# A float32 kernel of two transformer-like layers: convolution inputs turned by block transposes and transfers, a second queue of pieces, and smaller edits at the gates, the middle, the opening and the end

## The chip, the cores and the metric

The kernel runs on one core of a Trainium2 chip. The metric is the device time of one execution in microseconds, lower is better. A core has TensorE (PE in the profile; PEld is its weight load), VectorE (DVE), ScalarE (ACT), GpSimd (POOL) and SyncE (SP), which in this kernel issues nearly all DMA transfers.

## What is computed

A sequence of 256 tokens of width 2048, all in float32, goes through three blocks. The first is a gated MLP with mixing over tokens, the second a stick-breaking attention; neither is touched by the change, apart from the first instructions of the kernel. The third block is the one that matters here. Cut to its core, it is:

```python
xn = rmsnorm(x, norm_mix_pre)                       # 256 x 2048
mq, mk, mv, mo, mi, mf, aq, ak, av, g_m, g_a = split_cols(xn @ w_in)
# mq, mk, mv, mo, aq, ak, av: 1024 columns each; mi, mf: 4 each; g_m, g_a: 2048 each
qk = silu(causal_depthwise_conv(concat(mq, mk), conv_w, conv_b))   # 4 taps over tokens
h  = mlstm_chunkwise(*heads(qk), heads(mv), mi + i_bias, mf + f_bias)  # 4 heads of 256
h_m = rms_of_head(h) * mlstm_norm * sigmoid(mo)
h_a = attention(rope(aq), rope(ak), av)             # 8 heads of 128
merged = sigmoid(g_m) * (h_m @ w_branch_m) + sigmoid(g_a) * (h_a @ w_branch_a)
x = x + rmsnorm(merged @ w_out, norm_mix_post)
u = square(relu(rmsnorm(x, norm_ffn_pre) @ w_up))
x = x + rmsnorm(u @ w_down, norm_ffn_post)
```

The convolution is `out[t] = b + sum over j of w[j] * u[t - 3 + j]`, with zeros before the first token.

## The kernel before

**Matrix products in three passes.** Each float32 weight is split in two: the high half `t_wh` (written by ACT, line 42) and the low half `t_wl` (written by DVE, line 51, as the weight less its high half). Activations are held split and transposed, as `xth`/`xtl` (also `yth`/`ytl`, `mth`/`mtl`), and a product is the sum of three matmuls: low weights by high activations, high by high, and high by low. PE's work on them is line 33.

**Groups.** Weights come in groups of 128 x 1024 elements, 512 KB each, all in one order written in the program: SP loads a group to one of five buffers (`t_stage`), ACT and DVE split it into one of five pairs (`t_wh`, `t_wl`). Ahead of each group's matmuls `advance` emits the split of the group four later and the load of the next one. A load waits for the split that used its buffer, a split for the matmuls that used its pair. A usual group covers two row tiles of the activation and 512 columns of the weight, for two halves of the tokens (i = 0, 1): 12 matmuls. Eight such groups make a chunk of 512 output columns (`proj`). The gates have 8 columns only, 16 row tiles in two groups of 8 (`proj_gates`): there the weights, padded to 128 columns, are the stationary side and all 256 tokens are the moving side, three matmuls of 256 per row tile.

**Pieces.** All other work is cut into pieces, Python functions that emit instructions on the engines. They stand in a deque (`pieces`); `later(f, (g, 2), ...)` appends them, each with a least distance in groups from the piece before it, or from when it was queued. After each group `offer` emits the first piece if its distance has passed (and one more if over 18 stand in the queue); `need` emits pieces until a result that is wanted now is in the program. So the order on every engine is fixed when the program is built, and an engine that stands waiting in a piece holds back everything behind it on that engine, weight splits included.

**The third block before the change.** The order of chunks of `w_in` is: q columns of c = 0, gates, k columns of c = 0, v and o columns of c = 0, then q, k, v, o of c = 1, then q, k, v of the attention (c = 0, 1), then the branch products and so on. After each q or k chunk of the recurrent part `conv_t` queues four pieces. `first` (distance 2) transposes two 128 x 128 blocks for both halves of the tokens on PE (four transposes, line 36), ACT copies them behind three zero columns to `pad`, and DVE does the four taps of the first block (`tensor_scalar`, line 48, and three `scalar_tensor_tensor`, line 54). `second` does the taps of the other block, then ACT takes the tanh of half of it, and DVE multiplies (silu with a factor of two) into `vreg`. Both twice per chunk. The gates' pieces (`piece`, `gates_one` to `gates_five`) come from `gates_in`; the heads of the recurrence (`h0`, `h1`, `start`, `end`) are queued after the q, k, v and o chunks of a c. A rotary embedding is two pieces (`piece(0)`, `piece(1)`), the turn of its result for the attention a third (`turn_part`, which calls `send_heads`), and the scores follow five groups after them.

**Turning by block transposes.** Other chunks are already transposed without PE: `turn_chunk` makes 32 x 32 block transposes of both halves on DVE (line 39, `STREAM_TRANSPOSE`), and `send_turned` moves the blocks by four DMA transfers on SP to their places.

**Middle.** The last chunk of `w_out` is emitted so that its last three groups end with 18 matmuls for the first half of the tokens, then 18 for the second (`halves`, `late_groups=3`). Then come five small matmuls on constants, both square sums, the transposes of x (set up by `to_xt_now`), the norm and updates of the first half (`half_norm(0)`, `x3(0, 0, ..)`, `x3(1, 0, ..)`), the norm and updates of the second, and the products with `w_up`.

**End.** `last_norm(0)`, updates of chunks 0 to 2 of the first half, `last_sum(1)` (the last square sum), `update(3, 0)`, `last_norm(1)` and the updates of the second half.

**Opening.** ACT's first instruction is an activation on a zeroed tile; SP's first DMAs are `norm_g`, the first part of x (`load_x(0)`) and then weights and further parts of x in turn.

Of the kernel before, what the change touches and what calls it, by code (L numbers as in the profile page):

```python
# [16 lines left out]
D = 2048  # L17
# [162 lines left out]
def _program(nc, A, out, ctx):  # L180
# [30 lines left out]
    pad, _ = sb("pad", [128, 2, 260], offset=s_at + 4096)  # L211
    cpb, _ = sb("cpb", [128, 4 * 130], offset=s_at)
    ubuf, _ = sb("ubuf", [128, 2, 2, 512], offset=s_at)
    hold, _ = sb("hold", [8, S], offset=s_at + 4096 + 2112)
# [45 lines left out]
    pieces = deque()  # L260
    group_at = [0]
    pumped_at = [0]

    def pump():
        assert pieces, "nothing to pump"
        pumped_at[0] = group_at[0]
        pieces.popleft()[0]()
# [4 lines left out]

    def later(*fs):

        for f in fs:
            f, n = f if isinstance(f, tuple) else (f, 1)
            pieces.append((f, n, group_at[0]))
# [35 lines left out]
    AC.do(lambda e: e.activation(junk[:, 0:64], blank[:, 0:64], ACT.Copy), c_blank)  # L313
# [24 lines left out]
    def load_x(n):  # L338
        part = slice(256 * max(0, 2 * n - 2), 256 * max(1, 2 * n)) if n != 1 else slice(256, 512)
        x_in.append(SP.dma(lambda e: e.dma_start(hres[:, :, part], xin[:, :, part]), s_x[n], 16))  # L340
# [8 lines left out]
    load_x(0)  # L349
# [51 lines left out]
    def split_group(j):  # L401
        marks = (used[j - N_SPLIT],) if j >= N_SPLIT else ()
        s, r = j % N_STAGE, j % N_SPLIT
        src, hi, lo = stage[:, s], wh[:, r], wl[:, r]
        a = AC.do(lambda e: e.activation(hi, src, ACT.Copy), loaded[j], *marks)
        split_hi.append(a)
        split.append(DV.do(lambda e: e.tensor_tensor(lo, src, hi.bitcast(F32), ALU.subtract), a, *marks))
# [49 lines left out]
    def proj(xh, xl, k0, ready, halves=None, late_groups=1, high=None):  # L457
# [5 lines left out]
        for g in range(nk // 2):  # L463
# [24 lines left out]
            if halves is not None and g >= nk // 2 - late_groups:  # L488
                if g == nk // 2 - late_groups:
# [5 lines left out]
                    halves.append(mark)  # L495
                mark = group_products(xh, xl, k0, pair, n, nk, j, g, 1, ready, True)
# [47 lines left out]
    def proj_gates(xh, xl, ready):  # L544
# [5 lines left out]
        for g in range(2):  # L550
# [4 lines left out]
            for kk in range(8):  # L555
# [706 lines left out]
    def conv_t(src, mark, dst, base, marks, done):  # L1262
# [12 lines left out]
        for b in range(2):  # L1275
            s = {}

            def first(b=b, s=s):
# [16 lines left out]
                if b == 1:  # L1295
                    done(tp)
# [523 lines left out]
    for c in range(3):  # L1820
        update(c, 0)
# [61 lines left out]
```

How the kernel before makes its waits and increments, by code:

```python
    def wait(self, *marks):  # L87
        for sem, value in marks:
            if self.seen.get(sem.name, 0) < value:
                self.seen[sem.name] = value
                self.items.append(lambda e, s=sem, v=value: e.wait_ge(s, v))
# [1 line left out]
    def do(self, emit, *marks):  # L93
        self.wait(*marks)
        self.n += 1
        f = emit(BOUND)
        self.items.append(lambda e: f(e).then_inc(self.sem, 1))
        return (self.sem, self.n)
# [5 lines left out]
    def dma(self, emit, sem, value, *marks):  # L105
        self.wait(*marks)
        f = emit(BOUND)
        self.items.append(lambda e: f(e).then_inc(sem, 16))
        return (sem, value)
```

## Time and profile before

| | us |
|---|---|
| median of 3 runs (2595.32 to 2595.67) | 2595.36 |
| the profiled execution, its own time | 2595.48 |
| its span in the trace | 2593.7 |
| PE busy | 2583.2 (100%) |
| PEld busy | 2142.4 (83%) |
| DVE busy | 1599.8 (62%) |
| ACT busy | 1231.5 (47%) |
| POOL busy | 20.8 (1%) |

The span runs from the first to the last instruction of the trace; the execution's own time has 1.8 us more around it. Busy times are sums over the span. PE's weight loads overlap its matmuls. In rows of time order a matmul of 512 columns shows 0.39, since matmuls are pipelined; the distance from one to the next is 0.227. The DMA engines moved 203 GB/s on the mean. Where an engine sat idle before an instruction, the row has in brackets how long and which instruction released it.

### The profile page before, as it was taken

To read this page: it belongs to the slowest core of one execution; us is meant where nothing else is said; L and a number is where in the kernel's file an instruction comes from. 1 tells how busy PE (TensorE), PEld (TensorE's weight loads), DVE (VectorE), ACT (ScalarE), POOL (GpSimd) and SP (SyncE) were. 2 spreads that over 40 slices of the span, in tenths; PEclk is the share of its full clock that TensorE was granted. 3 is DMA by queue.
4 is the path that set the end of the run, shared out by engine and by line. 5 is a ranking of instruction groups with operands and counts; after the bars stand their busy time and mean duration, and the time that the engine had idled before them with its cause. 6 is when DMAs were issued, how large, how long until landed. Compare 5 with 4: busy or idle time off the path is not lost.

```text
span 2593.7 us, 29783 instructions
## 1 busy us (share of the span) xinstructions
PE 2583.2 (100%) x11589; PEld 2142.4 (83%) x11589; DVE 1599.8 (62%) x1851; ACT 1231.5 (47%) x1468; POOL 20.8 (1%) x46
## 2 busy tenths in 40 slices
PE   9999999999999999999999999999999999999999
PEld 7888888888888888888888888888878888888887
DVE  5546565566665656676866776556576565565565
ACT  6554443444545555455544444444454344444443
POOL 1000000000000000000000000000000000000000
PEclk9999999999999999999999999999999999999999
DMA  8667766676777777787555777666667676676674
GB/s 272 184 195 207 203 205 192 200 205 196 213 219 203 205 212 194 217 231 216 169 174 161 219 217 213 203 203 201 198 178 220 194 205 216 188 217 206 198 222 146
DMA packets 526205, 526.40 MB, mean 203 GB/s; under 512 B 286432, under 2 KB 289104, under 8 KB 526064
## 3 DMA queue, kind: packets, MB, share of 16 engines
q1 hardware_dynamic: 523536, 517.30, 67.7%
q0 software_dynamic: 2384, 6.93, 1.2%
q8 instruction: 91, 1.49, 0.2%
q14 instruction: 50, 0.41, 0.0%
q10 hardware_dynamic: 144, 0.26, 0.0%
HBM read 488.24 MB, written 2.10 MB: 189 GB/s over the span
## 4 chain that ended last, share of the span: by engine, by line
PE 99%; DVE 0%; ACT 0%; DMA 0%; issue 0%; SPq 0%; ACTq 0%
PE bank L33 98%; PE bank L36 1%; DMA t_hres<-in_x_dram 0%; DVE t_hres L54 0%; DVE t_xtl L54 0%; ACT t_xth L42 0%; DVE t_wl L51 0%; ACT t_wh L42 0%; ACT t_junk L42 0%; DVE t_vreg L51 0%; DVE t_pool L51 0%; ACT t_rq L42 0%; ACT t_vreg L42 0%; DVE t_scl L63 0%; DVE t_rq L54 0%
## 5 line engine op out<-in xcount | busy, mean ns | idle before, releaser
L51 DVE TENSOR_TENSOR t_wl<-t_stage,t_wh 128x1024 fp32r<-128x1024 f32 x914 | 1107.9, 1221 | 778.1 <-ACT t_wh L42 775.2
L42 ACT ACTIVATE t_wh<-t_stage 128x1024 fp32r<-128x1024 f32 x914 | 961.4, 1058 | 992.9 <-PE bank L33 983.5
L33 PE MATMUL bank<-t_wl,t_xth 128*128 128x512 f32 x2496 | 978.7, 392 | 0.6 <-DVE t_wl L51 0.6
L33 PE MATMUL bank<-t_wh,t_xtl 128*128 128x512 f32 x2496 | 971.3, 389 | 0.0
L33 PE MATMUL bank<-t_wh,t_xth 128*128 128x512 f32 x2496 | 971.2, 389 | 0.0
L33 PEld LDWEIGHTS bank<-t_wl,t_xth 128*128 128x128 f32 x2496 | 468.8, 188 | 97.9 <-DVE t_wl L51 1.4
L33 PEld LDWEIGHTS bank<-t_wh,t_xtl 128*128 128x128 f32 x2496 | 468.5, 188 | 98.1 <-DVE t_wl L51 0.5
L33 PEld LDWEIGHTS bank<-t_wh,t_xth 128*128 128x128 f32 x2496 | 468.9, 188 | 96.4 <-issue 0.2
L33 PE MATMUL bank<-t_wl,t_yth 128*128 128x512 f32 x1024 | 398.8, 389 | 0.0
L33 PE MATMUL bank<-t_wh,t_yth 128*128 128x512 f32 x1024 | 398.4, 389 | 0.0
L33 PE MATMUL bank<-t_wh,t_ytl 128*128 128x512 f32 x1024 | 398.3, 389 | 0.0
L33 PEld LDWEIGHTS bank<-t_wh,t_ytl 128*128 128x128 f32 x1024 | 192.2, 188 | 40.0
L33 PEld LDWEIGHTS bank<-t_wh,t_yth 128*128 128x128 f32 x1024 | 192.2, 188 | 39.9
L33 PEld LDWEIGHTS bank<-t_wl,t_yth 128*128 128x128 f32 x1024 | 192.2, 188 | 39.8
L42 ACT ACTIVATE t_pool<-bank,t_scl 128x512 f32<-128x512 f32 x120 | 76.1, 686 | 94.8 <-PE bank L33 93.1
L39 DVE STREAM_TRANSPOSE t_pool<-t_pool 128x512 f32<-128x512 f32 x96 | 99.0, 1072 | 0.0
L54 DVE SCALAR_TENSOR_TENSOR t_ytl<-t_ytl,t_yth 128x1024 fp32r<-128x1024 f32 x32 | 39.2, 1225 | 49.6 <-ACT t_yth L42 49.6
L42 ACT ACTIVATE t_yth<-t_ytl 128x1024 fp32r<-128x1024 f32 x32 | 33.9, 1060 | 56.9 <-DMA t_ytl<-t_pool 56.6
L33 PE MATMUL bank<-t_wl,t_mth 128*128 128x512 f32 x128 | 49.8, 389 | 0.0
L33 PE MATMUL bank<-t_wh,t_mth 128*128 128x512 f32 x128 | 49.8, 389 | 0.0
L33 PE MATMUL bank<-t_wh,t_mtl 128*128 128x512 f32 x128 | 49.8, 389 | 0.0
L51 DVE TENSOR_TENSOR t_pool<-t_pool 128x1024 f32<-128x1024 f32 (+1 forms) x36 | 31.3, 870 | 25.1 <-ACT t_pool L42 23.3
(208 smaller groups left out, 866.9 us busy)
## 6 DMA issues: line engine op xcount, KB each, us to landing
t_stage<-in_a_w_in_dram SPq DMA_DIRECT2D x192, 512.0 KB, 4.4
t_stage<-in_w_in_dram SPq DMA_DIRECT2D x178, 512.0 KB, 4.3
t_stage<-in_b_w_in_dram SPq DMA_DIRECT2D x128, 512.0 KB, 4.5
t_stage<-in_w_up_dram SPq DMA_DIRECT2D x128, 512.0 KB, 3.8
t_stage<-in_w_down_dram SPq DMA_DIRECT2D x128, 512.0 KB, 4.2
t_stage<-in_a_w_out_dram SPq DMA_DIRECT2D x64, 512.0 KB, 4.2
t_ytl<-t_pool SPq DMA_DIRECT2D x128, 128.0 KB, 3.1
t_stage<-in_b_w_out_dram SPq DMA_DIRECT2D x32, 512.0 KB, 4.9
```

Of the source, the lines that this page charges most:

```text
L33: return lambda e: e.matmul(*a, **k)
L36: return lambda e: e.transpose(*a, **k)
L39: return lambda e: e.transpose(out, in_)
L42: return lambda e: e.activation(*a, **k)
L51: return lambda e: e.tensor_tensor(*a, **k)
L54: return lambda e: e.scalar_tensor_tensor(*a, **k)
```

## The change

- Two queues of pieces: `pieces`, as before, and `side`, filled by `beside`. Each has its own distances, counted from its own last piece. `offer` emits at most one piece after a group, from `side` first; `pump` likewise. A piece can carry a condition besides its distance.
- `conv_t` no longer uses PE. `send` turns a chunk by `turn_chunk` and `send_turned`; the taps follow four groups later, read the turned chunk directly at shifted ranges (the last tap over all 256 tokens, those before it from their shift on) and write to `smooth`. Squashing and product are in pieces of their own kind: the tanh is issued at the end of `two` and `four`, its product at the start of `three` and in `five`. These pieces go to `side`.
- Rotary and turning pieces of the attention go to `side`; the scores have a condition (both parts sent, five groups since) in place of their distance, and the first head of the recurrence has one too.
- Gates: the high and low halves of the 8 columns stand side by side in `wh` as 16 columns, and two matmuls per row tile take the place of three; the two rows of sums are added after their transposes.
- Middle: square sum, norm and updates of the first half are emitted between the two halves of the last chunk's matmuls.
- End: `update(3, 0)` ahead of `last_sum(1)`.
- Opening: `load_x(0)` is issued on ACT ahead of its first activation, and no longer on SP.

The diff, cut to what the prediction speaks of:

```diff
+    def queue(lane, fs):
+        for f in fs:
+            f = f if isinstance(f, tuple) else (f,)
+            lane.append((f[0], f[1] if len(f) > 1 else 1, group_at[0], f[2] if len(f) > 2 else None))
...
+    def beside(*fs):
+
+        queue(side, fs)
+
+    def due(lane, name):
+        return allowed(lane) and group_at[0] - max(pumped_at[name], lane[0][2]) >= lane[0][1]
 
     def offer():
-        if pieces and group_at[0] - max(pumped_at[0], pieces[0][2]) >= pieces[0][1]:
-            pump()
-            if len(pieces) > 18:
-                pump()
+        if due(side, "side"):
+            run_piece(side, "side")
+        elif due(pieces, "main"):
+            run_piece(pieces, "main")
+            if len(pieces) > 18 and allowed(pieces):
+                run_piece(pieces, "main")
...
+    load_x(0, AC)
+    AC.do(lambda e: e.activation(junk[:, 0:64], blank[:, 0:64], ACT.Copy), c_blank)
...
+        if gates:
+            src, hi = (slot(x, n, 128)[:, :, 0:8] for x, n in ((stage, s), (wh, r)))
+            lo = slot(wh, r, 128)[:, :, 8:16]
         split.append(DV.do(lambda e: e.tensor_tensor(lo, src, hi.bitcast(F32), ALU.subtract), a, *marks))
...
+                    if first_half is not None:
+                        first_half(acc[2 * pair], mark)
...
-                w_h, w_l = slot(wh, j % N_SPLIT, 128)[:, kk], slot(wl, j % N_SPLIT, 128)[:, kk]
-                PE.run(lambda e: e.matmul(o, w_l, all_tokens(xh, k), start=(k == 0), stop=False))
-                PE.run(lambda e: e.matmul(o, w_h, all_tokens(xh, k), start=False, stop=False))
-                mark = PE.do(lambda e: e.matmul(o, w_h, all_tokens(xl, k), start=False, stop=(k == 15)))
+                w_both = slot(wh, j % N_SPLIT, 128)[:, kk]
+                PE.run(lambda e: e.matmul(o, w_both, all_tokens(xh, k), start=(k == 0), stop=False))
+                mark = PE.do(lambda e: e.matmul(o, w_both, all_tokens(xl, k), start=False, stop=(k == 15)))
...
+        def send():
+            n, z, free = temps.take()
+            zv = z.rearrange("p x y -> p (x y)")
+            turned = turn_chunk(lambda i: src[:, i, :], zv, (mark, *free))
+            done(turned)
+            st["n"], x, free = temps.take()
+            st["x"] = x.rearrange("p x y -> p (x y)").rearrange("p (h s) -> p h s", h=4)
+            st["a"] = send_turned(zv, st["x"].rearrange("p h (i a s) -> p a (h i) s", i=2, a=4), turned, *free)
+            temps.give(n, st["a"])
+
+        def taps(h):
+            ch = base + h
+            x, y = st["x"][:, h, :], smooth[:, h % 2, :]
+            m = DV.do(lambda e: e.tensor_scalar(y, x, cw[:, 48 + ch:49 + ch], gc[:, 80 + ch:81 + ch],
+                                                ALU.mult, ALU.add), st["a"], *smooth_free[0])
+            for back in range(1, 4):
+                m = DV.do(lambda e, back=back: e.scalar_tensor_tensor(
+                    out=y[:, back:256], in0=x[:, 0:256 - back],
+                    scalar=cw[:, 48 - 16 * back + ch:49 - 16 * back + ch], in1=y[:, back:256],
                     op0=ALU.mult, op1=ALU.add), m)
-            return m
-
-        for b in range(2):
-            s = {}
-
-            def first(b=b, s=s):
-                n, t, free = trans.take()
-                for j in range(2):
-                    for i in range(2):
-                        f = lambda e, j=j, i=i: e.transpose(t[:, 256 * j + 128 * i:256 * j + 128 * i + 128],
-                                                            src[:, i, 128 * (2 * b + j):128 * (2 * b + j) + 128],
-                                                            ident)
-                        if i == 1 and j == 1:
-                            tp = PE.do(f)
-                        else:
-                            PE.run(f, mark, *free)
-                a = AC.do(lambda e: e.activation(pad[:, :, 3:259], t.rearrange("p (h s) -> p h s", h=2), ACT.Copy),
-                          tp, pad_mark, *pad_free[0])
-                trans.give(n, a)
-                s["n"], s["t"], s["free"] = temps.take()
-                s["a"] = a
-                taps(0, b, s)
-                if b == 1:
-                    done(tp)
-
-            def second(b=b, s=s):
-                m = taps(1, b, s)
-                x, th = s["t"][:, 0, :], s["t"][:, 1, :]
-                pad_free[0] = (m,)
-                a = AC.do(lambda e: e.activation(th, x, ACT.Tanh, scale=0.5), m)
-                v = DV.do(lambda e: e.scalar_tensor_tensor(
-                    out=dst[:, 512 * b:512 * b + 512], in0=th, scalar=1.0, in1=x, op0=ALU.add, op1=ALU.mult), a)
-                temps.give(s["n"], v)
-                marks.append(v)
-            later((first, 2), second)
+            st["m"] = m
+
+        y = smooth.rearrange("p h s -> p (h s)")
+
+        def squash(b):
+            st["t"] = AC.do(lambda e: e.activation(dst[:, 512 * b:512 * b + 512], y, ACT.Tanh, scale=0.5), st["m"])
+
+        def product(b):
+            out = dst[:, 512 * b:512 * b + 512]
+            v = DV.do(lambda e: e.scalar_tensor_tensor(out=out, in0=out, scalar=1.0, in1=y, op0=ALU.add,
+                                                       op1=ALU.mult), st["t"])
+            smooth_free[0] = (v,)
+            marks.append(v)
+
+        def one():
+            taps(0)
+
+        def two():
+            taps(1)
+            squash(0)
+
+        def three():
+            product(0)
+            taps(2)
+
+        def four():
+            taps(3)
+            temps.give(st["n"], st["m"])
+            squash(1)
+
+        def five():
+            product(1)
+        return (send, 1), (one, 4), two, (three, 2), four, (five, 2)
...
-        later((h0[0], 3), (h0[1], 2), start, h0[2], h1[0], h1[1], h1[2], end)
+        later((h0[0], 1, lambda: len(qk_marks) == 4), (h0[1], 2), start, h0[2], h1[0], h1[1], h1[2], end)
-            conv_t(t, a, dst, 8 * part + 4 * c, qk_marks, lambda tp, n=n: temps.give(n, tp))
+            beside(*conv_t(t, a, dst, 8 * part + 4 * c, qk_marks, lambda tp, n=n: temps.give(n, tp)))
-        later(lambda: piece(0), (lambda: piece(1), 2))
+        beside(lambda: piece(0), (lambda: piece(1), 2))
-        return ha, ((score, 5), highest, both((soften, 0)), both((soften, 1), (send, 0)),
+        return ha, ((score, 1, lambda: len(sent) == 2 and group_at[0] - sent[1] >= 5), highest, both((soften, 0)), both((soften, 1), (send, 0)),
...
+    def first_half(bank, mark):
+        sqm.append(square_sum(bank, ssq[:, 0, 3:4], mark))
+        half_norm(0)
+        x3(0, 0, 0, 2)
+        x3(1, 0, 0, 2)
...
+    update(3, 0)
     last_sum(1)
-    update(3, 0)
```

## Rows read from the trace of the kernel before

**Rows 1.** Who waited for whom on PE: us in total, times, longest.

```profile
PE bank L36 <- DVE t_hres L54: 3.1, 1, 3.1
PE bank L33 <- DVE t_wl L51: 0.6, 2, 0.4
```

**Rows 2.** PE's instructions in order of time: start, us, what.

```profile
1279.09 0.39 PE L33 MATMUL bank<-t_wl,t_xth 128*128 128x512 f32 x1
```

**Rows 3.** DVE's instructions in order of time, taps and products of the convolution.

```profile
1252.31 0.41 DVE L48 TENSOR_SCALAR t_pool<-t_pad,t_cw,t_gc 128x256 f32<-128x256 f32 x1
...
1254.20 1.22 DVE L51 TENSOR_TENSOR t_wl<-t_stage,t_wh 128x1024 fp32r<-128x1024 f32 x1
...
1275.84 0.69 DVE L54 SCALAR_TENSOR_TENSOR t_vreg<-t_pool 128x512 f32<-128x512 f32 x1 [0.70 <-ACT t_pool L42]
1276.79 2.36 DVE L51 TENSOR_TENSOR t_wl<-t_stage,t_wh 128x1024 fp32r<-128x1024 f32 x2 [0.26 <-ACT t_wh L42]
```

**Rows 4.** PE in order of time: first product of the gates, first after.

```profile
1203.38 0.28 PE L33 MATMUL bank<-t_xth,t_wl 128*128 128x256 f32 x1
...
1209.13 0.40 PE L33 MATMUL bank<-t_wl,t_xth 128*128 128x512 f32 x1
```

**Rows 5.** The chain that ended last: one set of the convolution's transposes.

```profile
1247.40 0.44 PE bank L36 x4
```

**Rows 6.** DVE and ACT in order of time: turns, rotary, heads' end.

```profile
1329.38 2.07 DVE L39 STREAM_TRANSPOSE t_pool<-t_pool 128x512 f32<-128x512 f32 x2
...
1337.77 1.06 ACT L42 ACTIVATE t_yth<-t_ytl 128x1024 fp32r<-128x1024 f32 x1 [2.44 <-DMA t_ytl<-t_pool]
...
1421.08 0.16 DVE L48 TENSOR_SCALAR t_hsm<-t_hsm 128x4 f32<-128x4 f32 x1
...
1423.66 1.68 DVE L54 SCALAR_TENSOR_TENSOR t_pool<-t_pool,t_hsm,t_vreg 128x256 f32<-128x256 f32 x4
...
1440.82 0.42 DVE L51 TENSOR_TENSOR t_pool<-t_pool,t_cosb 128x256 f32<-128x256 f32 x1
```

**Rows 7.** DVE and PE in order of time, the middle.

```profile
1876.67 2.59 DVE L51 TENSOR_TENSOR t_wl<-t_stage,t_wh 128x1024 fp32r<-128x1024 f32 x2 [3.93 <-ACT t_wh L42]
...
1881.71 0.15 DVE L54 SCALAR_TENSOR_TENSOR t_gsm<-t_ssq,t_gsm 128x1 f32<-128x1 f32 x1
...
1883.46 1.97 PE L36 MATMUL bank<-t_ident,t_hres 128*128 128x128 f32 x8 [3.09 <-DVE t_hres L54]
```

**Rows 8.** Stretches: length, busy PE, PEld, DVE, ACT, POOL, clock, DMA, GB/s.

```profile
1880.00:1885.00 5.00, 1.91 (x9) 1.54 (x8) 3.32 (x11) 0.59 (x3) 0.00 (x0) 0.81 0.47 171
...
2585.00:2590.00 5.00, 3.46 (x12) 1.73 (x10) 4.21 (x11) 1.33 (x4) 0.00 (x0) 1.00 0.39 150
```

**Rows 9.** DVE in order of time, the end.

```profile
2585.34 0.69 DVE L51 TENSOR_TENSOR t_vreg<-t_vreg,bank 128x512 f32<-128x512 f32 x1 [0.68 <-PE bank L33]
2586.07 0.69 DVE L51 TENSOR_TENSOR t_pool<-t_vreg,t_rowb 128x512 f32<-128x512 f32 x1
...
2587.34 0.15 DVE L54 SCALAR_TENSOR_TENSOR t_gsm<-t_ssq,t_gsm 128x1 f32<-128x1 f32 x1
```

**Rows 10.** All engines in order of time, the opening (SPq issues a transfer).

```profile
0.81 1.28 ACT L42 ACT_TABLE_LOAD   x1 [0.81 <-PEq L1871]
...
1.26 0.42 SPq L72 DMA_DIRECT2D t_hres<-in_x_dram  x1
```

**Rows 11.** DVE in order of time, gates two, four and five.

```profile
1223.75 0.17 DVE L45 COPY t_gsm<-bank 128x16 f32<-128x16 f32 x1 [0.69 <-PE bank L33]
...
1242.40 0.16 DVE L51 TENSOR_TENSOR t_gsm<-t_gsm,t_hsm 128x4 f32<-128x4 f32 x1 [1.83 <-ACT t_hsm L42]
...
1248.89 1.23 DVE L51 TENSOR_TENSOR t_dt<-t_dt,t_tri 128x1024 f32<-128x1024 f32 x1 [1.13 <-ACT t_dt L42]
```

**Rows 12.** The stretch of gates two to five; columns as in Rows 8.

```profile
1223.75:1250.04 26.29, 26.29 (x115) 21.02 (x115) 19.44 (x47) 10.93 (x15) 0.00 (x0) 1.00 0.50 148
```

**Rows 13.** The same, t_wl alone: length, DVE busy, clock, DMA share, GB/s.

```profile
1223.75:1250.04 26.29, 7.24 (x7) 1.00 0.50 148
```

More of the change, by code:

```diff
@@ L260, in _program, with allowed, run_piece @@
     pieces = deque()
+    side = deque()
     group_at = [0]
-    pumped_at = [0]
-    def pump():
-        assert pieces, "nothing to pump"
-        pumped_at[0] = group_at[0]
-        pieces.popleft()[0]()
+    pumped_at = {"main": 0, "side": 0}
+    def allowed(lane):
+        return lane and (lane[0][3] is None or lane[0][3]())
+    def run_piece(lane, name):
+        pumped_at[name] = group_at[0]
+        lane.popleft()[0]()
+    def pump():
+        if allowed(side):
+            run_piece(side, "side")
+        else:
+            assert allowed(pieces), "nothing to pump"
+            run_piece(pieces, "main")
     def need(have):
@@ L1146, in gates_in @@
         pair, o, m = proj_gates(xth, xtl, x_ready)
-        gt = hold[0:8, :]
-        a = AC.do(lambda e: e.activation(gt, o[0:8, :], ACT.Copy), m)
+        gt = hold[0:16, :]
+        a = AC.do(lambda e: e.activation(gt, o[0:16, :], ACT.Copy), m)
         acc_free[pair] = (a,)
@@ L1152, in piece @@
             n, t, free = misc.take()
-            PE.run(lambda e: e.transpose(t[:, 0:8], gt[:, 0:128], ident[0:8, 0:8]), a, *free)
-            tp = PE.do(lambda e: e.transpose(t[:, 8:16], gt[:, 128:256], ident[0:8, 0:8]))
+            PE.run(lambda e: e.transpose(t[:, 0:16], gt[:, 0:128], ident[0:16, 0:16]), a, *free)
+            tp = PE.do(lambda e: e.transpose(t[:, 16:32], gt[:, 128:256], ident[0:16, 0:16]))
+            sums = DV.do(lambda e: e.tensor_reduce(gat.rearrange("p i h -> p (i h)"),
+                                                   t[:, 0:32].rearrange("p (i part h) -> p i h part", i=2, part=2),
+                                                   AX, ALU.add), tp)
             for i in range(2):
                 mk = DV.do(lambda e, i=i: e.scalar_tensor_tensor(
-                    out=gat[:, i, :], in0=t[:, 8 * i:8 * i + 8], scalar=s12[:, i:i + 1], in1=gb,
-                    op0=ALU.mult, op1=ALU.add), tp, M["s12"], late["bias"])
+                    out=gat[:, i, :], in0=gat[:, i, :], scalar=s12[:, i:i + 1], in1=gb,
+                    op0=ALU.mult, op1=ALU.add), sums, M["s12"], late["bias"])
             misc.give(n, mk)
@@ L1590, in soft_chunk @@
         qk_marks = []
+        sent = []
         for part, dst in enumerate((q, k)):
@@ L1661, in _program, with half_norm, x3 @@
     xM = gsm[:, 11, 2:4]
+    x_high = {}
+    sqf = []
+    x3_marks = {}
+    m_sM = {}
+    def half_norm(i):
+        m_sM[i] = short_norm(sM[:, i:i + 1], xM[:, i:i + 1], partM[:, i:i + 1], ssq[:, i, 3:4], rq[:, 0, i:i + 1], D,
+                             (sqm[-1], m_part))
+    def x3(c, i, b0, nb):
+        part = slice(512 * c + 256 * b0, 512 * c + 256 * (b0 + nb))
+        m = DV.do(lambda e: e.scalar_tensor_tensor(
+            out=hres[:, i, part], in0=mo[:, i, part], scalar=sM[:, i:i + 1], in1=hres[:, i, part], op0=ALU.mult,
+            op1=ALU.add), m_sM[i], mo_marks[c], x2_marks[c])
+        for b in range(b0, b0 + nb):
+            x3_marks[c, b] = m
+    def first_half(bank, mark):
[3 more added lines that the diff above has]
+        x3(1, 0, 0, 2)
     for c in range(4):
@@ L1671, in _program @@
             misc.give(warm_n)
-        for i in range(2):
-            sqm.append(square_sum(ps[i], ssq[:, i, c:c + 1], m if halves is None else halves[i]))
+        for i in range(2) if c < 3 else (1,):
+            sqm.append(square_sum(ps[i], ssq[:, i, c:c + 1], m))
         if c == 2:
```

60 lines of the change are left out of this document (18 added, 42 removed).

## Prediction, made before the change was run

> **What bounds the kernel now.** I read the table of engines first, then who waited for whom on PE, then PE's, DVE's and ACT's instructions in order of time around each edit. PE is busy in all of the span and the engine waits are short: 3.1 us in the middle, at the normalisation before the feed-forward block, 0.6 for split weights [rows 1]. With the opening and the tail that is all that is not matmul work. So the bound is PE's own list of instructions, and an edit pays if it takes instructions off PE, or shortens opening, middle or end.
>
> But PE's cover has a thin spot that these views don't show. DVE writes the low half of each weight group (t_wl), four groups ahead. A group of 12 matmuls takes 2.72 us of PE (12 at 0.227, the step between matmuls). In the convolution stage DVE is the slower of the two for a while. I number the stage's groups from 0, so that the two groups of the gates are 8 and 9; then group 34 starts at 1279.09 [rows 2]. Counting t_wl against groups, its own is the first of the pair from 1276.79 to 1279.15 and ends at about 1278.0 [rows 3]. Only 1.1 us of cover is left there, where DVE may be three or four groups ahead. That decides the forecast.
>
> **The change, part by part.**
>
> *Gates.* 48 products of 256 columns run from 1203.38 to 1209.13 [rows 4], 0.12 each. 32 are left: 16 x 0.12 = **-1.9**. The smaller split of the two gate groups, one more reduction of some 0.2 and transposes of 16 rows instead of 8 lie on DVE or cost PE under 0.1; taken at nothing.
>
> *Transposes of the convolution.* Eight sets of four leave PE, 0.44 each [rows 5]: **-3.5**. Eight copies leave ACT. In their place DVE turns four chunks by two block transposes, 2.1 [rows 6], and SP issues 16 transfers. These wait on SP behind weight loads that have been released by then; SP issues the next load after them, and loads run five groups ahead. A turned chunk of this kind was waited for until 1337.77, 6.3 after its transposes ended at 1331.45 [rows 6]; the first tap follows four groups later (10.9), so no tap waits.
> The Trainium skill, VectorE: DVE Perf Modes, "The three transpose paths", warns that a plain strided DMA copy used as a transpose is 19 times slower than the DMA engine's own transposing path, and sends 128x128 turns to TensorE. By it the landings would be the bound; the measured 6.3 decides against it.
>
> *Middle.* The last chunk of w_out ends with 18 products for the first half of the tokens, then 18 for the second. Before, both norms came after all of that on ACT and DVE. Now the first half's square sum, norm and two updates run while PE does the second half. Their 1.4 on DVE push its last two t_wl (2.59, from 1876.67) by some 0.8, so that these end near 1880.05 instead of 1879.26. Then the second norm and its first update take the 1.75 that stand between 1881.71 and PE's start at 1883.46 [rows 7]: PE starts near 1881.8, 1.7 sooner. It has then been idle 1.4 instead of 3.1. The granted clock was 0.81 from 1880 to 1885, around the 3.1; it was 1.00 in the tail, where PE was busy for 3.46 of 5, idle for 1.5 in all [rows 8]. If it stays at 2.4 GHz, eight transposes (1.97 [rows 7] against 2 x 0.44 [rows 5]) and the first matmuls give back about 1.3 more. I take **-3.0**, bounds -1.7 and -3.3.
>
> *End.* One update stood between the second sum, whose product ended at 2586.76 (2586.07 + 0.69), and the second norm at 2587.34. It moves into the 0.68 that DVE idles before the last sum [rows 9]. **-0.5**, bounds 0 and -0.6.
>
> *Opening.* The first part of x was issued on SP at 1.26, behind norm_g [rows 10]. From ACT it can go at 0.81, and SP's weight loads all move up by one slot. PE, ACT and DVE wait for these loads in turn: **-0.4**, bounds 0 and -0.5. But ACT's first instruction is a table load of 1.28; the row doesn't tell whether that stands ahead of the transfer. If so, x is issued at 2.1 (0.81 + 1.28) and the opening costs +0.8.
> The Trainium skill, ScalarE: Activation LUTs, "What happens when an `exp` ACTIVATE runs", says that the compiler puts the table load right before the ACTIVATE that needs it; by that rule the transfer goes first, and no row here shows an ACT transfer ahead of a load.
>
> *The two queues.* Every group may offer one piece, now from either queue, each by its own gap. I count the pieces by group. Before: gates at 12 to 21, taps of the first q/k chunks at 23 to 33. After: send 11, gates 12 and 13, taps 15 and 16, gates 17, taps 18 and 19, gates 20, 21 product, send 22, gates 23 and 25, taps 26, 27, 29, 30. So DVE's work comes in one pack and is over by 32, where PE reaches these groups 1.9 and then 1.8 sooner. Ledger of DVE, from where it last was ahead to t_wl 34. t_wl 18 ended at 1223.06 before, 0.69 ahead of the copy at 1223.75 [rows 11]; now at 1223.06 - 1.9 = 1221.2.
> 16 t_wl by 1.18 = 18.9; eight tap sets, 1252.31 to 1254.20, 1.89 each = 15.1; three products by 0.69 = 2.1 [rows 3]; one send 2.1. Gates two to five: DVE was busy 19.4 in the stretch that holds them [rows 12], 7.2 of it t_wl [rows 13], and idled 1.83 and 1.13 inside them for ACT [rows 11]: 12.2 + 3.0 = 15.2. Four tanhs: each holds ACT until the taps are done, with the next weight split behind it on ACT: before, 0.70 idle + 0.69 product + 0.26 idle = 1.65 from taps to the next t_wl [rows 3]. The product is now a later piece, so all 1.65 is idle: 6.6. Sum 60.0: t_wl 34 is ready at 1281.2. PE would be there at 1279.1 - 1.9 - 1.8 = 1275.4. **PE waits 5.8** in all by group 34.
> A second pack (groups 43 to 51: send, end of the first heads 4.2 (1421.08 to 1425.3, the same piece for the second heads [rows 6]), four tap sets, the turn for the output 2.1, a product, two tanhs) is 10 x 1.18 + 2.1 + 4.2 + 7.6 + 2.1 + 0.7 + 3.3 = 31.8 of DVE in 10 groups of 2.72 = 27.2; I put the cover left by the heads, where PE has 1 to 2.6 us of other work in a piece, at 3 to 4: **+1.4**, bounds 0 and 3.
> A third is at groups 75 to 88: rotary pieces of six operations by 0.42, 2.5 [rows 6], used to follow the end of the second heads and now lie among it: four of these 10.0, the end of heads 4.2, three turns 6.3, one division with its wait for a landing, allowed at 4, and 14 x 1.18 = 16.5, in all 41.0 in 14 x 2.72 = 38.1. **+2.4**, an estimate; and the scores wait **+1.1** for k to land, since their five groups count from the issue while DVE is some 10 late. Bounds 0 and 7 for the two.
>
> **Sum.** -1.9 - 3.5 - 3.0 - 0.5 - 0.4 = -9.3; +5.8 + 1.4 + 3.5 = +10.7; together +1.4. The profiled execution took 2595.48 (span 2593.7, 1.8 around it), 0.1 over the median of 2595.36: 2595.5 + 1.4 = 2596.9, **2597**. The savings are eaten by DVE.
>
> **The rivals.**
> *A. The cover holds.* PE never waited in the convolution stage before, even with 1.1 left, and all that DVE's total gains is four sends, 8.4. If the packs spread by more than I count, no wait appears: 2595.4 - 9.3 = 2586. Against it: PE arrives 3.7 sooner at a spot with 1.1 of cover, so that 2.6 of wait stands even with DVE's old order. Half the waits give 2591.5.
> *B. Slower: the scores catch DVE's lag.* PE takes the q.k products in order, and the gate counts five groups (13.6) from the issue of the last turn. With DVE L behind, 2.1 + L + 5.5 to 6.3 must fit: it decides from L = 6. At L = 12, which the first pack reaches, each of the two attention chunks would hold PE 6 to 7: one of them at full price gives 2603. For it: landings of 6.3, rotary pieces of 2.5 among heads. Against: the second chunk has room again.
> *C. The transfer stands behind the table load:* +1.2 on the forecast, 2598.4.
>
> **Chances.** Forecast 0.55, its own range 2590 to 2601.5; A 0.20, B 0.17, C 0.08. Range 2587 to 2603: it leaves out A's full gain, and B where both chunks pay. A measurement of this kernel can tell 0.2% (5.2 us) from no change: faster means under 2590.2, slower over 2600.6. Faster: A and 0.04 of the forecast, 0.24. Slower: B and 0.03 of the others, 0.20. Same: the rest, 0.56.
>
> **What would show it.** PE's waits must name t_wl at groups 27 to 34 with 5 to 7 us, again near 55 and 81 to 87; no waits there is A. One wait of several us on the attention scores for a landing is B. Gates 3.8 instead of 5.75. In the middle PE idle 1.4 and a clock of 1.00; 0.8 means only -1.7. Three updates before the last sum grown to four. The first x transfer on ACT at 0.8, or 2.1 for C. I am wrong if DVE has idle stretches for want of PE between groups 20 and 34.

## The result and the profile after

The changed kernel takes 2600.65 us (median of 15 runs, 2599.84 to 2601.32) against 2595.6 for the one before in the same jobs (15 runs, 2593.76 to 2598.62): a ratio of 1.0019, 95% interval 1.0012 to 1.0026. The interval leaves out 1: the change costs 5.05, or 0.19%, which is just inside the 0.2% that the prediction counts as no change. The forecast was 2597, range 2587 to 2603. The span of the changed kernel is 2598.9 against 2593.7, +5.2.

Who waited for whom on PE, changed kernel (us in total, times, longest); they answer to [rows 1]:

```profile
PE bank L33 <- DVE t_wl L51: 10.0, 8, 4.3
...
PE bank L36 <- DVE t_hres L54: 1.1, 1, 1.1
```

The wait in the middle fell from 3.1 to 1.1, and the one for split weights grew from 0.6 to 10.0. The 0.6 are two waits in the opening, which the changed kernel has too (0.25 and 0.39); the other six, 9.4 in all, are in the third block, at groups 29, 31 and 34 (3.9 together), 55 (1.0), 82 and 86 (4.5). To see where the 5.2 came from I set the start of each group's first matmul in the changed trace against its start before, with the prediction's group numbers:

```
group      before   changed   difference
0         1181.62   1180.83    -0.79   opening
10        1209.13   1206.42    -2.71   gates (8, 9)
34        1279.09   1279.61    +0.52   first pack
45        1319.31   1319.95    +0.64   after the first heads
78        1421.31   1421.57    +0.26   after the second heads
85        1440.35   1441.74    +1.39
86        1443.07   1448.91    +5.84
87        1445.79   1454.20    +8.41
90        1453.95   1462.75    +8.80
241       1875.32   1884.13    +8.80   last group before the middle
250       1910.58   1916.26    +5.67
497       2582.42   2588.10    +5.68   last chunk
span      2593.7    2598.9     +5.2
```

The groups shown are ones at which PE has done the same work in both kernels, so that the difference moves only where something was gained or lost (at others, such as 94 or 100, it is 2.6 higher for a while, because the changed kernel does a piece of PE's work earlier). Between groups 10 and 45, and again between 45 and 78, it holds two things at once: the waits and the transposes that have left PE. Experiment e6, which has no waits there, shows 1.9 for each of the two sets of transposes. So the sum is -0.8 (opening) -1.9 (gates) -3.9 (transposes) -3.1 (middle) -0.5 (end) = -10.2, and +5.3, +1.6 and +8.5 for three packs of waits, +15.4. A pack is more than its waits (3.9, 1.0 and 4.5): around each wait some 0.3 more go, since the row's idle begins only when the last matmul's 0.39 is over and the first matmul afterwards takes longer; waits under 0.15 aren't listed; and in the third pack there is the clock, below.

The gates, PE in order of time, changed kernel: first of 32 products, and the first matmul after them, 3.83 later against 5.75 [rows 4].

```profile
1202.59 0.28 PE L33 MATMUL bank<-t_xth,t_wh 128*128 128x256 f32 x1
...
1206.42 0.40 PE L33 MATMUL bank<-t_wl,t_xth 128*128 128x512 f32 x1
```

The middle, DVE and PE in order of time, changed kernel ([rows 7] before): the two updates of the first half, the two t_wl pushed behind them, the first update of the second half, PE's start.

```profile
1884.90 1.41 DVE L54 SCALAR_TENSOR_TENSOR t_hres<-t_mixout,t_scl,t_hres 128x512 f32<-128x512 f32 x2
1886.23 2.35 DVE L51 TENSOR_TENSOR t_wl<-t_stage,t_wh 128x1024 fp32r<-128x1024 f32 x2
...
1889.70 0.88 DVE L54 SCALAR_TENSOR_TENSOR t_hres<-t_mixout,t_scl,t_hres 128x256 f32<-128x256 f32 x2
...
1890.25 1.09 PE L36 MATMUL bank<-t_ident,t_hres 128*128 128x128 f32 x8 [1.08 <-DVE t_hres L54]
```

Stretches of the changed kernel (columns as in Rows 8), around the middle and then around group 86:

```profile
1885.00:1890.00 5.00, 4.17 (x19) 3.21 (x17) 4.59 (x10) 2.40 (x5) 0.00 (x0) 1.00 0.26 74
1890.00:1895.00 5.00, 4.62 (x26) 3.80 (x27) 3.77 (x8) 2.56 (x6) 0.00 (x0) 1.00 0.39 136
```

```profile
1440.00:1444.00 4.00, 4.00 (x19) 3.31 (x18) 0.00 (x0) 0.00 (x0) 0.00 (x0) 1.00 0.81 169
1444.00:1448.00 4.00, 0.62 (x3) 0.19 (x1) 1.59 (x2) 3.56 (x5) 0.00 (x0) 1.00 0.80 302
1448.00:1452.00 4.00, 3.09 (x7) 2.48 (x8) 3.79 (x8) 3.40 (x4) 0.00 (x0) 0.52 0.46 131
1452.00:1456.00 4.00, 4.00 (x13) 3.11 (x12) 3.79 (x9) 1.06 (x1) 0.00 (x0) 0.63 0.65 167
```

The granted clock stays at 1.00 over the middle, where it was 0.81 before [rows 8], and the eight transposes take 1.09 instead of 1.97. At group 86 it is the other way round. PE is idle for 4.3, and then the clock is 0.52 and 0.63 in the two stretches from 1448. In the stretch from 1440 to 1444 DVE and ACT do nothing at all while the DMA engines are 0.81 busy: ACT waits for a transfer, and DVE for ACT.

What ACT waits for is in these rows of groups 82 to 86: SP's issues, ACT, DVE and PE in order of time, changed kernel.

```profile
1431.91 3.15 SPq L72 DMA_DIRECT2D t_vreg<-t_pool  x4
1435.11 0.69 SPq L72 DMA_DIRECT2D t_stage<-in_w_in_dram  x1
1435.90 4.75 SPq L72 DMA_DIRECT2D t_ytl<-t_pool  x4
```

```profile
1429.99 1.07 ACT L42 ACTIVATE t_wh<-t_stage 128x1024 fp32r<-128x1024 f32 x1 [1.66 <-PE bank L33]
1444.44 1.06 ACT L42 ACTIVATE t_yth<-t_ytl 128x1024 fp32r<-128x1024 f32 x1 [13.38 <-DMA t_ytl<-t_pool]
1445.41 1.25 ACT L42 ACTIVATE t_pool<-bank,t_scl 128x512 f32<-128x512 f32 x2
1446.55 4.85 ACT L42 ACTIVATE t_wh<-t_stage 128x1024 fp32r<-128x1024 f32 x5
```

```profile
1432.91 2.05 DVE L39 STREAM_TRANSPOSE t_pool<-t_pool 128x512 f32<-128x512 f32 x2
1434.89 3.45 DVE L51 TENSOR_TENSOR t_wl<-t_stage,t_wh 128x1024 fp32r<-128x1024 f32 x3
1445.53 1.23 DVE L54 SCALAR_TENSOR_TENSOR t_ytl<-t_ytl,t_yth 128x1024 fp32r<-128x1024 f32 x1 [7.19 <-ACT t_yth L42]
1447.63 1.23 DVE L51 TENSOR_TENSOR t_wl<-t_stage,t_wh 128x1024 fp32r<-128x1024 f32 x1 [0.88 <-ACT t_wh L42]
```

```profile
1448.91 0.79 PE L33 MATMUL bank<-t_wl,t_xth 128*128 128x512 f32 x1 [4.29 <-DVE t_wl L51]
1449.51 0.63 PE L33 MATMUL bank<-t_wh,t_xth 128*128 128x512 f32 x1
1449.93 0.63 PE L33 MATMUL bank<-t_wh,t_xtl 128*128 128x512 f32 x1
```

ACT reaches the division of the second heads' turned output and stands for 13.38, with five weight splits behind it (the x5 at 1446.55). DVE turned that chunk at 1434.96. SP issued it from 1435.90 to 1440.65, behind the turned rotary chunk, and it was there at 1444.4: 9.5 after the turn, against 6.3 and 6.7 for the two such chunks in the kernel before. There ACT stood 2.85 at the same division:

```profile
1437.45 1.06 ACT L42 ACTIVATE t_yth<-t_ytl 128x1024 fp32r<-128x1024 f32 x1 [2.85 <-DMA t_ytl<-t_pool]
```

PE uses up the groups already split, waits 4.3 at group 86, and then works at half the clock: matmuls 0.43 apart instead of 0.227, so that group 86 takes 5.29 instead of 2.72. The page TensorE: Matmul & The Clock Gate of the Trainium skill, section "What's actually happening", has a throttled state at half the clock that the array falls back to when PE idles; this trace agrees with 0.52 behind an idle of 4.3.

The first pack: ACT in order of time, changed kernel, at the two tanhs of the k chunk.

```profile
1266.98 0.64 ACT L42 ACTIVATE t_vreg<-t_smooth 128x512 f32<-128x512 f32 x1 [4.28 <-DVE t_smooth L54]
1267.52 2.94 ACT L42 ACTIVATE t_wh<-t_stage 128x1024 fp32r<-128x1024 f32 x3
1276.62 0.63 ACT L42 ACTIVATE t_vreg<-t_smooth 128x512 f32<-128x512 f32 x1 [6.16 <-DVE t_smooth L54]
1277.16 3.89 ACT L42 ACTIVATE t_wh<-t_stage 128x1024 fp32r<-128x1024 f32 x4
```

The same shape: ACT waits 4.28 and 6.16 for DVE's taps, and three and four splits stand behind it.

End and opening, changed kernel: DVE's four updates ahead of the second sum and the second norm ([rows 9] before); then the opening, where ACTq issues the first part of x before ACT loads its table ([rows 10] before).

```profile
2588.27 2.74 DVE L54 SCALAR_TENSOR_TENSOR t_hres<-t_pool,t_scl,t_hres 128x512 f32<-128x512 f32 x4
...
2591.74 0.69 DVE L51 TENSOR_TENSOR t_pool<-t_vreg,t_rowb 128x512 f32<-128x512 f32 x1
2592.50 0.16 DVE L54 SCALAR_TENSOR_TENSOR t_gsm<-t_ssq,t_gsm 128x1 f32<-128x1 f32 x1
```

```profile
0.82 0.46 ACTq L72 DMA_DIRECT2D t_hres<-in_x_dram  x1
...
1.31 1.28 ACT L42 ACT_TABLE_LOAD   x1 [1.31 <-PEq L1918]
```

### The profile page after: what moved, and what is told of

Read it like the earlier page. It is cut to its first block, busy times and chain, and to the rows that moved or that the text cites. A ratio compares the mean times of both kernels' runs of the same rounds, so it can differ in the third digit from the quotient of the medians.

```text
span 2598.9 us, 29709 instructions
## 1 busy us (share of the span) xinstructions
PE 2581.4 (99%) x11541; PEld 2136.6 (82%) x11541; DVE 1604.5 (62%) x1859; ACT 1228.9 (47%) x1460; POOL 21.0 (1%) x46
## 4 chain that ended last, share of the span: by engine, by line
PE 95%; DVE 3%; ACT 1%; issue 1%; DMA 0%; SPq 0%; ACTq 0%; DVEq 0%
PE bank L33 94%; DVE t_wl L51 1%; DVE t_smooth L54 0%; ACT t_wh L42 0%; PE bank L36 0%; DVE t_pool L39 0%; DMA t_hres<-in_x_dram 0%; SPq L72 0%; DVE t_pool L48 0%; DMA t_ytl<-t_pool 0%; DVE t_pool L51 0%; ACT t_pool L42 0%; DVE t_hres L54 0%; ACT t_junk L42 0%; DVE t_smooth L48 0%
## 5 line engine op out<-in xcount | busy, mean ns | idle before, releaser
L33 PE MATMUL bank<-t_wl,t_xth 128*128 128x512 f32 x2496 | 980.0, 393 | 10.2 <-DVE t_wl L51 10.0
L39 DVE STREAM_TRANSPOSE t_pool<-t_pool 128x512 f32<-128x512 f32 x104 | 107.5, 1072 | 0.0
```

The source lines that it names most:

```text
L33: return lambda e: e.matmul(*a, **k)
L39: return lambda e: e.transpose(out, in_)
```

## The experiments

Eleven runs of ten kernels follow (e11 is e6 again). "Packs" are PE's losses by the table of group starts, at groups 10 to 45, 45 to 78 and 78 to 98, each run against the kernel before, with 1.9 for the transposes added back where they have left PE. A trace is one execution, and its group starts are compared with the one trace of the kernel before.

```
                             median us   ratio to before [95%]      packs
changed kernel                2600.65    1.0019 [1.0012, 1.0026]    5.3  1.6  8.5
e5 four edits only            2589.59    0.9976 [0.9966, 0.9985]    0    0    0
e1 tanh later                 2593.36    0.9992 [0.9982, 1.0001]    0    0    7.7
e3 rotary in main queue       2592.87    0.9988 [0.9978, 0.9997]    5.2  2.3  0
e6 both of these              2585.80    0.9962 [0.9947, 0.9976]    0    0    0
e4 division later             2594.58    0.9994 [0.9985, 1.0004]    5.2  1.3  1.7
e7 turn apart                 2593.89    0.9992 [0.9982, 1.0001]    5.2  1.8  1.1
e2 product with tanh          2597.02    1.0006 [0.9996, 1.0015]    3.1  0.6  7.4
e8 PE convolution, side       2600.97    1.0019 [1.0009, 1.0028]    6.2  5.1  0
e9 e8 with tanh later         2593.74    0.9994 [0.9985, 1.0003]    2.5  1.6  0
e10 before, more warm         2594.43    0.9994 [0.9985, 1.0003]    0    0    0
e11 e6 again                  2585.77    0.9960 [0.9947, 0.9972]    0    0    0
```

**e5, the four edits without queues and turning.** The changed kernel with `conv_t`, `pad` and the order of pieces as before.

> Gates, middle, end and opening as changed; convolution, pieces and their one order as before the change. The changed kernel's trace, group by group against the one before, books the opening at -0.8, the gates at -1.9, the middle at -3.1 and the end at -0.5. Theory (the four edits are sound and only the two queues and the turned convolution cost): these four add up to -6.3, less a wait of 0 to 0.9 at group 34, where PE comes 1.9 sooner to a cover of 1.1: 2589.3 to 2590.2, and no wait for split weights over 1 us. Rival (an early PE uncovers waits elsewhere, so part of the four is given back even without the queues): 2592 or more, with new waits after the gates.

It took 2589.59, in the theory's range. Its only waits for split weights are those of the opening, and the cover of 1.07 at group 34 was still 1.05 although PE came 2.3 sooner: DVE's pieces there follow PE, so they came sooner too. The four edits are sound, and what the queues and the turned convolution cost is 11.1.

**e1, tanh later.**

```diff
+    soon = []
     def offer():
+        while soon:
+            soon.pop(0)()
...
             taps(1)
-            squash(0)
+            soon.append(lambda: squash(0))
```

> The changed kernel, with each tanh of the convolution emitted one group later than its last taps; everything else keeps its group. Theory (the first two packs of waits exist because ACT stands at the tanh with the next weight split behind it, so that DVE idles 1.65 a time): DVE gains 4 x 1.65 = 6.6 by group 34, more than the 5.1 that PE waits there, and the 1.4 near group 55 goes too, while the 8.5 at groups 81 to 87 stay: 2600.6 - 6.5 = 2594.1, first pack under 1. Rival (DVE simply has too much in one pack and the idle is not what decides): at least 3 of the 5.1 stay, 2597 to 2599.

2593.36, as the theory had it: the first two packs are gone to the last tenth. Of the 4.9 that PE still waits, 0.6 are in the opening and 4.3 in the third pack. Waits on PE, e1, and the same tanh on ACT:

```profile
PE bank L33 <- DVE t_wl L51: 4.9, 4, 4.2
```

```profile
1263.78 0.64 ACT L42 ACTIVATE t_vreg<-t_smooth 128x512 f32<-128x512 f32 x1 [3.33 <-DVE t_smooth L54]
```

ACT still stands 3.33 there, but the next group's split is now ahead of the tanh, so that DVE has a t_wl to do meanwhile, and nobody pays for the stand.

The third pack is 7.7 here instead of 8.5. PE idles 4.17 at group 86 instead of 4.29, but the low clock behind it costs less: group 86 takes 4.2 instead of 5.29. On the other side PE, which comes sooner, waits 0.52 for the landing of a turned rotary chunk at the scores (at 1457.82), which it didn't in the changed kernel.

**e3, rotary pieces in the main queue.**

```diff
-        beside(lambda: piece(0), (lambda: piece(1), 2))
+        later(lambda: piece(0), (lambda: piece(1), 2))
...
-            beside(turn_part)
+            later(turn_part)
```

> The changed kernel, with the rotary and turning pieces of the attention in the main queue again, behind the heads' end, turn and division. Theory (the 8.5 at groups 81 to 87 come from ACT standing at the division until a turned chunk lands that was issued behind another turned chunk): that chunk goes out alone, lands some 5.5 to 6.5 after its turn instead of 9.5, and the 8.5 fall to 0 to 0.5: 2592.1 to 2592.6; the first pack keeps its 5.1. Rival (DVE has fallen behind by the two queues' total and pays wherever the pieces are put): half of the 8.5 or more comes back elsewhere, 2596 or more.

2592.87, 0.3 over the theory's range; the third pack is nothing, and the second grew by 0.7, most of it a wait of 0.80 for split weights at group 66. ACT at the division, e3:

```profile
1434.64 1.06 ACT L42 ACTIVATE t_yth<-t_ytl 128x1024 fp32r<-128x1024 f32 x1 [4.88 <-DMA t_ytl<-t_pool]
```

It stands 4.88 instead of 13.38, which the cover holds.

**e6, both.**

> The two changes together: tanh one group later, rotary pieces back in the main queue. Theory: all three packs go, 2600.6 - 5.1 - 1.4 - 8.5 = 2585.6, and this beats the kernel before by 10. Rival (the packs share one cause, a total of DVE work): the gains don't add, 2589 or more.

2585.80, and 2585.77 as e11, 0.9960 of the kernel before. e1 alone gains 7.3 and e3 alone 7.8, together 14.9: the causes are separate and add up. This is the fastest version.

**e4 and e7, which part of the third pack is which.** e4 sets `gap=6` in the two `to_xt` of the recurrent part; e7 has `beside((turn_part, 4))` for `beside(turn_part)`.

> The changed kernel, with the division of the recurrent part's two turned outputs six groups after their turn instead of three. Theory (at the division ACT stands until the chunk lands, and every weight split behind it): the chunk has landed when ACT comes to it, so of the 8.5 at groups 81 to 91 only what DVE's pack itself causes stays, about 1.1 at groups 81 to 84 and up to 1 more: 2593 to 2595. Rival (DVE's total of work there is the cause, not ACT's stand): 6 or more of the 8.5 stay, 2598 or more.

> The changed kernel, with each turn of a rotary result four groups after its rotary pieces instead of one, so that the turned output of the second heads is issued ahead of it and not behind it. Theory (a turned chunk that is issued within 4 us of another lands some 4 later than one alone): it lands 5.5 to 6.5 after its turn instead of 9.5, and its turn itself comes 2.1 sooner; of the 8.5 some 2.5 to 4 stay: 2594.5 to 2596.5. Rival (landings are as long as they are; ACT's stand alone matters): only the 2.1 are gained, 2598.5.

e4 took 2594.58, with 1.7 of the third pack left: DVE's work is all there, only ACT no longer stands at the division. It stands 4.49 (until 1444.80) for a weight load that was issued behind the two turned chunks on SP, with two shorter such waits behind it, but the cover holds. So the two chunks delay the weight loads as well, at no cost here. e7 took 2593.89, 0.6 better than the theory's best. SP's issues and ACT at the division, e7:

```profile
1433.96 3.47 SPq L72 DMA_DIRECT2D t_ytl<-t_pool  x4
1437.47 1.44 SPq L72 DMA_DIRECT2D t_stage<-in_w_in_dram  x2
1439.09 5.84 SPq L72 DMA_DIRECT2D t_vreg<-t_pool  x4
```

```profile
1439.95 1.06 ACT L42 ACTIVATE t_yth<-t_ytl 128x1024 fp32r<-128x1024 f32 x1 [7.95 <-DMA t_ytl<-t_pool]
```

Issued first, the output's chunk lands 6.0 after its turn (1433.93) and ACT stands 7.95; now the rotary chunk is the one that comes 9.1 after its turn, and nobody waits for it. The expectation had forgotten that 3.0 of the 8.5 are the low clock behind the idle of 4.3, and go with it. The turn itself came 1.0 sooner, not 2.1. e4 and e7 together: the stand is the cause, and the two chunks in a row are what made it long. What is left in e4 is 1.1 at groups 82 to 84, which is DVE's load, and 0.6 at the scores, where PE waits 0.35 for a rotary chunk to land; in e7 it is 0.3 at groups 82 to 84 and 0.8 around group 87.

**e2, product with its tanh.** `product(b)` moves from `three` and `five` to behind `squash(b)`.

> The changed kernel, with each product of the convolution in the same piece as its tanh, so that DVE does it while ACT comes to the next split, as before the change. Theory (the ledger's idle of 1.65 a tanh is filled by the product's 0.69): three products leave the ledger up to group 34, so the 5.1 fall by 2.1 to 3.0, and the 1.4 near group 55 by 0.7 to 1.4; the 8.5 stay: 2597.1 to 2597.9. Rival (products run in gaps that cost nothing where they stand now): 2600.6.

2597.02, 0.1 under the theory's range: the first pack fell by 2.2 (2.1 expected), the second by 1.0, the third by 1.1 (none expected). The first two agree with the ledger's idle at the tanh and its size. In the third, PE idles 3.72 instead of 4.29 at group 86, and that group then takes 4.3 instead of 5.29; 0.6 come back as a wait for a landing at the scores (0.39).

**e8 and e9, the side queue with the old convolution.** e8 is e5 with the convolution's pieces in the side queue, and with the first head of the recurrence released by its condition, as in the changed kernel, instead of its distance of three groups; e9 is e8 with tanh and product one group later.

```diff
-            later((first, 2), second)
+            beside((first, 2), second)
...
-        later((h0[0], 3), (h0[1], 2), start, h0[2], h1[0], h1[1], h1[2], end)
+        later((h0[0], 1, lambda: len(qk_marks) == 4), (h0[1], 2), start, h0[2], h1[0], h1[1], h1[2], end)
```

> The four edits, the rotary pieces in the main queue, and the old convolution on PE, its pieces in the side queue. Theory (the first two packs come from the turned convolution's sends and tanhs, not from having two queues): eight sets of transposes return to PE, +3.6 on 2585.8, and no wait for split weights over 1: 2589.2 to 2590. Rival (two queues put too much DVE work into one stretch, whatever the convolution is): 2 or more of waits for split weights at groups 12 to 34, 2591.5 or more.

> The kernel of e8 (old convolution on PE, its pieces in the side queue), with each tanh and its product emitted one group later. In e8 ACT stood for 8.64 us before the tanh at 1257.84 and for 9.09 before the one at 1331.42, each time with weight splits behind it. Theory (the waits come from ACT standing at a tanh for a DVE that is behind, and from nothing else in the density of the two queues): all of e8's waits go, those for split weights and the 3.5 of the transposes at 1347: 2589.2 to 2590.5. Rival (two queues put more DVE work in a stretch than the cover holds): half or more of the 11.4 between e8 and e5 stays, 2595 or more.

The theory of e8 fell. Same instructions as e5, in another order: 2600.97 instead of 2589.59. ACT at two tanhs, and PE's waits, e8:

```profile
1257.84 0.63 ACT L42 ACTIVATE t_pool<-t_pool 128x512 f32<-128x512 f32 x1 [8.64 <-DVE t_pool L54]
...
1331.42 0.63 ACT L42 ACTIVATE t_pool<-t_pool 128x512 f32<-128x512 f32 x1 [9.09 <-DVE t_pool L54]
```

```profile
PE bank L33 <- DVE t_wl L51: 3.6, 3, 2.9
PE bank L36 <- ACT t_pool L42: 3.5, 1, 3.5
```

Of the 3.6 for split weights 0.4 are in the opening, the rest at groups 29 and 31. With the 3.5 that makes 6.7 of waits in the third block; much of what is left of the 11.4 is the clock, which was 1.00 in e5 over both places: behind an idle of 2.91 at 1266.71 it was 0.57 from 1268 to 1272, and behind the 3.48 at 1347.00 it was 0.62 from 1347 to 1351.

e9 lies between its two theories. Its waits:

```profile
PE bank L33 <- DVE t_wl L51: 2.3, 3, 1.7
PE bank L36 <- ACT t_pool L42: 1.9, 1, 1.9
```

Of the 2.3, 0.6 are in the opening. Moving the tanh gives 7.2 of the 11.4 back: 3.1 of waits, and the rest for the greater part the clock, which stays at 1.00 behind the idles of 1.66 and 1.89. 4.2 stay. So the order that the side queue and the earlier head make costs by itself; ACT's stands at the tanhs make up most of it, but not all. That the 4.2 come from packing gates and taps is my reading, and no run takes the queue and the head's condition apart. The turned convolution is better off here than the one on PE: its pieces ask nothing of PE, so PE can't be caught by them (the 3.5 and 1.9 are transposes that wait for a chunk that ACT has not yet copied out of its accumulator). Against e11, e9 is 8.0 slower: 3.9 of transposes and these 4.2.

**e10, more warm matmuls before the middle.** The kernel before with `range(11)` for `range(5)`.

> The kernel before, with 11 instead of 5 small matmuls on constants between the last product of w_out and the norms in the middle. Theory (of the 3.1 gained in the middle some 1.3 are the clock, which was 0.81 and 0.85 in the two stretches from 1880 and 1.00 in the changed kernel): with PE idle for about 0.3 to 0.5 instead of 3.1 the clock stays at 1.00 and PE starts on time at full speed: 1.2 to 1.4 gained, 2594.3. Rival (the low clock follows the idle DVE and ACT chain, or the gain was all in the order of the norms): no gain, 2595.6.

2594.43 against 2595.76: 1.3 gained by the medians, and 1.07 in the trace between groups 241 and 250. The interval of the ratio reaches 1, but all 10 times lie under all 21 of the kernel before. PE's start, and the stretch from 1880, e10:

```profile
1883.73 1.09 PE L36 MATMUL bank<-t_ident,t_hres 128*128 128x128 f32 x8 [0.50 <-DVE t_hres L54]
```

```profile
1880.00:1885.00 5.00, 4.37 (x24) 3.40 (x23) 3.52 (x13) 0.78 (x3) 0.00 (x0) 1.00 0.51 180
```

Nothing about the norms was changed, PE starts where it did (the whole trace is 0.27 late from group 0 on), and still there is a gain: the clock's part of the middle's 3.1. The trace's 1.07 fits it, since the idle's part is 3.09 - 1.08 = 2.0.

**e11, e6 again.**

> The kernel of e6 again (tanh one group later, rotary pieces in the main queue), on this chip beside e9 and e10, for its size: 2585.8, 10.0 under the kernel before, and 3.6 under e9 if e9 has no waits, since its eight sets of transposes are what e11 takes off PE.

2585.77, ratio 0.9960 [0.9947, 0.9972].

## Why the prediction was right, and where its sum was wrong

The time lay in the range, 3.7 over the forecast and on the slower side of "no change", and the mechanism was the one forecast: some 10 gained, all of it and more eaten by waits for split weights in three packs, at the groups named. That the total came as near owes something to luck: the third pack lies outside its own bounds, and errors the other way took 1.4 of that back. Term by term:

- Gates: -1.9, measured -1.9.
- Transposes: -3.5, measured -3.9 (e6), 0.48 a set instead of 0.44. The slower matmuls behind each set were left out. The remark on strided copies doesn't bear on these transfers, which only move blocks that DVE has transposed; the four chunks landed 5.5 to 6.6 after their turns.
- Middle: -3.0, measured -3.1: PE idle 1.1 instead of 3.1, eight transposes in 1.09 instead of 1.97. That part of it is the clock was forecast, and e10 shows it; the part is 1.1, not 1.3. PE's start came 2.0 sooner, not 1.7.
- End: -0.5, measured -0.5.
- Opening: -0.4; the one trace of the changed kernel has -0.8, but the eleven traces with this opening have -0.03 to -0.79 at group 0, mean -0.37. The transfer is issued at 0.82 with the table load behind it at 1.31, so rival C is out. (Its price adds up to 2598.1, not 2598.4.)
- First pack: +5.8, measured +5.3, of which 3.9 are listed waits (5 to 7 were named as the sign). The ledger held: from t_wl 18 to t_wl 34 DVE took 59.1 against 60.0, with the four idles at tanhs at 1.65 each. It charged gates four with an idle of 1.83; in the changed trace that is 0.55, since ACT's table load now comes earlier, in a stand before a tanh. It also left the opening's gain out on both sides, which cancels. e1 and e2 show the ledger's largest and least certain line, the 1.65 idle at each tanh: without it the pack is 0, with the product filled in 3.1.
- Second pack: +1.4, measured +1.6, and 0 in e1.
- Third pack: +2.4 and +1.1, with bounds 0 and 7, measured +8.5. This is the step that failed. Its own figures, 41.0 against 38.1, give 2.9, and 2.4 was put down without a reason; but that is small beside the two things that were missing. First, "one division with its wait for a landing, allowed at 4" looked at DVE's time. It is ACT that stands, for 13.38, with all weight splits behind it, and DVE is idle for 7.19. That long a stand needs a landing of 9.5 after the turn, where I used the 6.3 of [rows 6]: in the kernel before no two turned chunks are issued within 4 us there, and I had written down myself that the rotary pieces, with three turns, now lie among the end of the heads. e3, e4 and e7 show it from three sides. Second, an idle PE has a price beyond its length: 4.3 of wait brought 2.6 more in the same group and 0.4 in the next, at the low clock. I had used just this effect as a gain in the middle and left it out as a cost here. The +1.1 at the scores did not come: the score piece stands five groups earlier than before (group 91 instead of 96) and waits for nothing. It comes in small where PE arrives sooner: 0.8 in e1, 0.6 in e2 and e4.
- Rival A (the cover holds) did not come; e6 makes it true, by moving the tanhs and the rotary pieces. Rival B had the side right and the place wrong: not the scores but the division caught DVE's lag.

The sum, +1.4, was thus 5.0 too low at the third pack (8.5 against 3.5) and 0.2 at the second, and too high by 0.5 at the first, 0.4 at the opening, 0.4 at the transposes and 0.1 in the middle: +5.2.

What stays open is what makes the 4.2 that e9 keeps over e5, and why the low clock behind nearly the same idle costs less in e1 than in the changed kernel.

## What to carry to other kernels

An instruction that waits on one in-order engine is priced by what stands behind it: here a tanh or a division of 0.6 to 1.1 us held three to five weight splits on ACT and starved two other engines. What counts is whether the stand uses up the cover: stands of 3.33 (e1) and 4.88 (e3) cost nothing. Count the cover, in groups already prepared, against the longest stand, and emit the waiting instruction one step later, behind the next step's bulk work: that move at the tanhs, and the rotary pieces back in the main queue, turned +5 into -10 us. When pieces of two queues are merged, list which of them now issue transfers within a few us of each other, and take landings from such pairs, not from lone ones.

## What the runs showed of the hardware

- A turned chunk of four transfers (128 KB each) lands 5.3 to 6.6 after its turn when alone in the changed kernel's third block (5.2 to 7.7 over all runs, and up to 8.1 just before the block, at 1164). The second of two turned some 3 to 4 us apart needs 9.5 and 8.7 in the changed kernel, 9.1 and 8.4 in e7, and 8.2 to 9.3 in e1, e2 and e4. SP needs 4.75 (changed kernel) and 5.84 (e7) to issue the four transfers of the second chunk, against 3.15 and 3.47 for the first.
- PE after an idle of 4.3 runs its next matmuls 0.43 apart instead of 0.227, for 5.7 us, which costs some 3.0. The clock was also low behind idles of 2.9 (e8, 0.57), 3.1 (kernel before, 0.81 and 0.85 over five us each) and 3.5 (e8, 0.62), and 1.00 behind those of 1.1 (middle), 1.7 and 1.9 (e9). It need not fall during the idle: in e8 PE worked from 1266.7 to 1268.1 at 1.00 after its 2.9, and from 1268.1 to 1271.5 at 0.50. Behind the idle of 1.7 in the first pack, at a clock of 1.00, a group took 2.89 instead of 2.72. In e10 eleven small matmuls on constants instead of five kept the clock at 1.00, for 1.1 in the trace.
- The span up to group 0 varies by 0.8 between traces of kernels that are alike up to there, so that an edit of the opening worth 0.4 can't be read from one trace.
